# Fifteen couples instead of twelve in the second half of the value stages, with two weight sums made by accumulating DMAs

## The reference

```python
def block(args):                         # routed experts; u and v are tables of 16384 rows
    ht, et, gt = args
    act = jax.nn.gelu(jnp.einsum('td,ted->te', ht, u[et]), approximate=False)
    return jnp.einsum('te,ted->td', gt * act, v[et])
...
for layer in range(DEPTH):               # 2
    h = rms_norm(x, ...)
    x = x + (even_mix if layer % 2 == 0 else fox_mix)(h, ...)
    h = rms_norm(x, ffn_norm[layer])
    x = x + peer_ffn(h, peer_wq[layer], peer_keys[layer], peer_u[layer], peer_v[layer])
```

## Time and profile before

| | before |
|---|---|
| median of 3 runs | 2184.07 us (2183.23 to 2188.88) |
| profiled execution, its own time | 2185.0 us |
| its span | 2183.3 us, granted TensorE clock 0.999 of full |
| TensorE busy | 2169.3 us, 14158 matmuls |
| VectorE, ScalarE, GpSimd busy | 1775.3, 1257.6, 725.2 us |
| DMA | 386.11 MB, mean 177 GB/s |

### The profile page before, as it was taken

How to read it: one execution, slowest core, us unless ns; L and a number is a source line. 1 busy time by engine, 2 the same in 40 slices (tenths; PEclk the granted TensorE clock), 3 DMA queues, 4 the chain that set the end, 5 groups by cost and what they waited for, 6 DMA issues and landing times.

```text
span 2183.3 us, 42549 instructions
## 1 busy us (share of the span) xinstructions
PE 2169.3 (99%) x14158; PEld 1890.7 (87%) x14158; DVE 1775.3 (81%) x3460; ACT 1257.6 (58%) x1935; POOL 725.2 (33%) x737
## 2 busy tenths in 40 slices
PE   9999999999999999999999999999999999999999
PEld 8899888888888888888988888888888888899887
DVE  8776885888899999866678678888999997658895
ACT  6556556555444666565565555554446665566764
POOL 1506886333345100002088853324440001530000
PEclk9999999999999999999999999999999999999999
DMA  5364555555565665354455555555656654444565
GB/s 176 100 200 156 190 186 182 173 173 173 177 211 179 205 210 193 127 183 144 165 175 191 185 180 171 172 169 191 211 175 213 202 181 160 155 145 155 189 187 163
DMA packets 109836, 386.11 MB, mean 177 GB/s; under 512 B 12544, under 2 KB 15008, under 8 KB 109472
## 3 DMA queue, kind: packets, MB, share of 16 engines
q1 hardware_dynamic: 106864, 382.34, 53.0%
q10 hardware_dynamic: 2864, 2.36, 0.3%
HBM read 383.46 MB, written 1.06 MB: 176 GB/s over the span
## 4 chain that ended last, share of the span: by engine, by line
PE 92%; DVE 4%; POOL 2%; DMA 1%; ACT 1%; issue 0%; SPq 0%; ACTq 0%; DVEq 0%; POOLq 0%
PE bank L2611 24%; PE bank L2583 13%; PE bank L2663 5%; PE bank L2665 5%; PE bank L2664 5%; PE bank L2706 3%; PE bank L2707 3%; PE bank L2708 3%; PE bank L2499 3%; PE bank L2487 3%; PE bank L3070 3%; PE bank L2491 3%; PE bank L2727 2%; PE bank L2728 2%; PE bank L2729 2%; PE bank L2853 1%
## 5 line engine op out<-in xcount | busy, mean ns | idle before, releaser
L670 ACT ACTIVATE w_hi<-ring 128x1024 fp32r<-128x1024 f32 x651 | 686.9, 1056 | 435.4 <-PE bank L2665 186.8
L1378 DVE TENSOR_TENSOR w_lo<-ring,w_hi 128x1024 fp32r<-128x1024 f32 x500 | 610.2, 1223 | 109.1 <-ACT w_hi L670 109.1
L2611 PE MATMUL bank<-x_parts,w_hi 128*128 128x512 f32 x2320 | 583.1, 393 | 0.3 <-ACT w_hi L670 0.3
L2611 PEld LDWEIGHTS bank<-x_parts,w_hi 128*128 128x128 f32 x2320 | 417.0, 189 | 74.9 <-issue 0.4
L554 POOL TENSOR_TENSOR w_lo<-ring,w_hi 128x1024 fp32r<-128x1024 f32 x151 | 364.5, 2420 | 265.1 <-DVE x_parts L1363 158.5
L566 POOL COPY quads<-sco 128x32 f16 (+1 forms) x256 | 227.1, 915 | 439.7 <-DVE sco L1917 439.6
L2583 PEld LDWEIGHTS bank<-x_parts,w_lo 128*128 128x128 f32 x2368 | 324.3, 190 | 25.1 <-DVE w_lo L1378 3.0
L2583 PE MATMUL bank<-x_parts,w_lo 128*128 128x256 f32 x2368 | 335.7, 283 | 0.2 <-DVE w_lo L1378 0.2
L2663 PE MATMUL bank<-w_hi,x_parts 128*128 128x512 f32 x512 | 201.7, 394 | 0.0
L2665 PE MATMUL bank<-w_lo,x_parts 128*128 128x512 f32 x512 | 199.6, 390 | 0.0
L2664 PE MATMUL bank<-w_hi,x_parts 128*128 128x512 f32 x512 | 199.1, 389 | 0.0
(11 more groups left out here) (418 smaller groups left out, 3812.9 us busy)
## 6 DMA issues: line engine op xcount, KB each, us to landing
ring<-u_dram SPq DMA_DIRECT2D x256, 512.0 KB, 3.3
ring<-v_dram SPq DMA_DIRECT2D x208, 512.0 KB, 3.3
big<-v_dram SPq DMA_DIRECT2D x48, 512.0 KB, 4.4
ring<-up_dram SPq DMA_DIRECT2D x44, 512.0 KB, 3.5
ring<-wq_dram SPq DMA_DIRECT2D x32, 512.0 KB, 4.2
ring<-sb_in_dram SPq DMA_DIRECT2D x31, 512.0 KB, 3.3
ring<-od_in_dram SPq DMA_DIRECT2D x25, 512.0 KB, 3.3
ring<-down_dram SPq DMA_DIRECT2D x22, 512.0 KB, 4.2
```

The source lines that it names most:

```text
L670: A(w_hi[:, k % RING, :], ring[:, k % RING, :], ACT.Copy).then_inc(g["w_hi_done"], 1)
L1378: V.tensor_tensor(w_lo[:, k % RING, :], ring[:, k % RING, :], w_hi[:, k % RING, :].bitcast(F32), ALU.subtract).then_inc(g["lo_dve"], 1)
L2611: mm(dst[:, :], hi[:, rows[c]], x_both[:, c, :], start=(c == 0), stop=False, skip_group_check=True)
```

## The change

The second half is laid out as 4 plain pieces and 15 couples with two plain pieces behind each: 34 plain pieces (40 before). A raw buffer now has five blocks instead of four: SyncE loads the block B12 twice, side by side, and behind the load GpSimd issues one DMA that adds the blocks B22 and B11 onto the two copies (128 x 1024, SBUF to SBUF, `accum_op=add`). The result is T3 and T1, which VectorE made before as `t13`. For the first two couples VectorE still makes them. The signs of the sums are turned so that adding fits. VectorE's `late_sums` is split into `activation_sums` (three pieces ahead, behind the low parts) and `weight_sums` (two pieces ahead; T2 and T4, waits for the accumulating DMA). Part 0 has 2560 columns instead of 1536, part 1 has 1024 instead of 2048. TensorE raises `pair_used` for the first time after five of a couple's products instead of three. The fold begins with bank 0 released earlier and adds into the output banks as soon as each term is there. The first pair of a layer is loaded four pieces later in the first half, and some semaphores for small tables are merged.

```diff
@@ -36,11 +36,11 @@
...
 UP = 2.0 ** 14
-HEAD, COUPLED, BETWEEN, TAIL = 4, 12, 3, 0
+HEAD, COUPLED, BETWEEN, TAIL = 4, 15, 2, 0
 DIRECT = HEAD + COUPLED * BETWEEN + TAIL
...
 EARLY_SUMS = ("t13", "t2", "t4", "s1", "s3", "s2", "s4")
-SUMS = ("t13", "s1", "t2", "s3", "s2", "t4", "s4")
+SUMS = ("s1", "s3", "s2", "s4", "t2", "t4")
@@ -140,11 +140,11 @@
-        pair_raw = [big[:, b * 4 * CB:(b + 1) * 4 * CB] for b in range(2)]
-        pair_sum = [big[:, 8 * CB:12 * CB], big[:, 12 * CB:16 * CB], sco[:, 4 * CB:8 * CB]]
-        pair_sum_low = [sums_low[:, 0:4 * CB], sums_low[:, 4 * CB:8 * CB], sco_rounded[:, 4 * CB:8 * CB]]
-        pair_hi = [(parts[:, 0:3 * CB], parts[:, 3 * CB:7 * CB]), (parts[:, 13 * CB:16 * CB], sco_rounded[:, 0:4 * CB])]
-        pair_lo = [parts[:, 7 * CB:10 * CB], parts[:, 10 * CB:13 * CB]]
+        pair_raw = [big[:, b * 5 * CB:(b + 1) * 5 * CB] for b in range(2)]
+        pair_sum = [big[:, 10 * CB:12 * CB], big[:, 12 * CB:14 * CB]]
+        pair_sum_low = [sums_low[:, 2 * CB:4 * CB], sums_low[:, 4 * CB:6 * CB]]
+        pair_hi = [(parts[:, 0:5 * CB], sco_rounded[:, 5 * CB:7 * CB]), (parts[:, 10 * CB:15 * CB], sums_low[:, 6 * CB:8 * CB])]
+        pair_lo = [parts[:, 5 * CB:10 * CB], sco_rounded[:, 0:5 * CB]]
         at_pair = 3 * 2 * T
@@ -349,7 +350,12 @@
         def pair_arrived(layer, s):
-            return pair_loaded[s % 2], 32 * (layer * ((COUPLED + 1 - s % 2) // 2) + s // 2 + 1)
+            of_both = (COUPLED + 1 - s % 2) // 2
+            return pair_loaded[s % 2], 48 * (layer * of_both + s // 2 + 1)
+
+        def pair_added(layer, s):
+
+            return pair_added_to[s % 2], 16 * (layer * ((COUPLED - 1 - s % 2) // 2) + s // 2)
         def pair_free(layer, s, half=2):
@@ -470,12 +476,14 @@
             def load_pair(layer, s):
                 k, raw = couple_row(s), pair_raw[s % 2]
-                for at, row in ((0, k + 1), (PIECE, k)):
-                    sp.dma_start(raw[:, at:at + PIECE], a[f"v{layer}"][row]).then_inc(pair_loaded[s % 2], 16)
+                upper = a[f"v{layer}"][k][:, CB:2 * CB].rearrange("p (o n) -> p o n", o=1).to_broadcast([P, 2, CB])
+                sp.dma_start(raw[:, 0:2 * CB], a[f"v{layer}"][k + 1]).then_inc(pair_loaded[s % 2], 16)
+                sp.dma_start(raw[:, 2 * CB:3 * CB], a[f"v{layer}"][k][:, 0:CB]).then_inc(pair_loaded[s % 2], 16)
+                sp.dma_start(b3(raw[:, 3 * CB:5 * CB], 2), upper).then_inc(pair_loaded[s % 2], 16)
             def first_pairs(layer):
-                sp.wait_ge(g["pieces_used"], starts[f"v{layer}"] + 16)
+                sp.wait_ge(g["pieces_used"], starts[f"v{layer}"] + 20)
                 load_pair(layer, 0)
@@ -483,13 +491,13 @@
...
                 for d in range(DIRECT):
+                    sp.wait_ge(*low_bits(k0 + d - RING))
+                    load(a[f"v{layer}"][direct_row(d)], k0 + d)
                     s = pair_after(d - 2)
...
                         load_pair(layer, s + 2)
-                    sp.wait_ge(*low_bits(k0 + d - RING))
-                    load(a[f"v{layer}"][direct_row(d)], k0 + d)
@@ -607,9 +615,14 @@
...
+                for s in range(2, COUPLED):
+                    raw = pair_raw[s % 2]
+                    pool.wait_ge(*pair_arrived(layer, s))
+                    pool.dma_start(raw[:, 3 * CB:5 * CB], raw[:, CB:3 * CB], accum_op=ALU.add).then_inc(pair_added_to[s % 2], 16)
+
                 if layer == 0:
                     pool.wait_ge(g["x_ready"], 4 * 2)
-                    pool.wait_ge(g["fox_rows_spread"], 16)
+                    pool.wait_ge(g["fox_rows_spread"], 32)
                     tab = fx_tab.rearrange("p (h c t) -> p h c t", h=FH, c=3)
@@ -1048,12 +1061,12 @@
...
                     direct_chunk(d)
-                    for ahead, parts in ((3, (0,)), (2, (1,)), (1, (2, 3))):
+                    for ahead, parts in ((1, (1, 2, 3)), (2, (0,))):
                         s = pair_after(d + ahead)
...
                                 pair_part(s, part)
-                act.wait_ge(*pair_free(layer, COUPLED - 1))
+                act.wait_ge(*pair_free(layer, COUPLED - 1, 1))
                 A(pair_ends[:, 0:CB], bank[0][:, :], ACT.Copy).then_inc(g["pair_high"], 1)
@@ -1760,18 +1773,17 @@
             def couple_blocks(s):
-                raw, out, row = pair_raw[s % 2], pair_sum[s % 3], couple_row(s) * T
-                b21, b22, b11, b12 = (raw[:, j * CB:(j + 1) * CB] for j in range(4))
-                t13, t1, t2, t4 = b3(out[:, 0:2 * CB], 2), out[:, CB:2 * CB], out[:, 2 * CB:3 * CB], out[:, 3 * CB:4 * CB]
-                b12_twice = b12.rearrange("p (o n) -> p o n", o=1).to_broadcast([P, 2, CB])
+                raw, out, row = pair_raw[s % 2], pair_sum[s % 2], couple_row(s) * T
+                b21, b22, b11, t3, t1 = (raw[:, j * CB:(j + 1) * CB] for j in range(5))
+                t2, t4, t13 = out[:, 0:CB], out[:, CB:2 * CB], raw[:, 3 * CB:5 * CB]
                 a11, a21, a12, a22 = (big[:, row + j * P:row + (j + 1) * P] for j in range(4))
                 s2, s1, s4 = (act_sum[s % 2][:, j * P:(j + 1) * P] for j in range(3))
-                return {"t13": (t13, b12_twice, b3(raw[:, CB:3 * CB], 2)), "t2": (t2, b22, t1), "t4": (t4, b21, t2),
-                        "s1": (s1, a21, a22), "s3": (a21, a21, a11), "s2": (s2, s1, a11), "s4": (s4, a12, s2)}
+                return {"t13": (t13, t13, raw[:, CB:3 * CB]), "t2": (t2, b22, t1), "t4": (t4, b21, t2),
+                        "s1": (s1, a22, a21), "s3": (a21, a11, a21), "s2": (s2, s1, a11), "s4": (s4, a12, s2)}
             def block_sum(blocks, name):
-                V.tensor_tensor(*blocks[name], ALU.add if name == "s1" else ALU.subtract).then_inc(g["pair_summed"], 1)
+                V.tensor_tensor(*blocks[name], ALU.subtract if name in ("s1", "s3", "s4") else ALU.add).then_inc(g["pair_summed"], 1)
             def early_weight_sums(layer, s):
@@ -1784,26 +1796,26 @@
...
-            def late_sums(layer, s):
+            def activation_sums(layer, s):
...
                 if s >= 2:
-                    dve.wait_ge(*pair_arrived(layer, s))
                     dve.wait_ge(*pair_free(layer, s - 2))
-                    block_sum(blocks, "t13")
                 block_sum(blocks, "s1")
-                if s >= 2:
-                    dve.wait_ge(*sums_done(layer, s, "t13"))
-                    block_sum(blocks, "t2")
                 dve.wait_ge(*sums_done(layer, s, "s1"))
...
                 block_sum(blocks, "s2")
-                if s >= 2:
-                    dve.wait_ge(*sums_done(layer, s, "t2"))
-                    block_sum(blocks, "t4")
                 dve.wait_ge(*sums_done(layer, s, "s2"))
                 block_sum(blocks, "s4")
+
+            def weight_sums(layer, s):
+
+                blocks = couple_blocks(s)
+                dve.wait_ge(*pair_added(layer, s))
+                block_sum(blocks, "t2")
+                dve.wait_ge(*sums_done(layer, s, "t2"))
+                block_sum(blocks, "t4")
             def experts(layer):
@@ -2017,34 +2029,44 @@
...
                     dve.wait_ge(*pair_high(layer, 4 * s + part + 1))
-                    dst, src, high = ((pair_lo[b], pair_raw[b][:, 0:3 * CB], pair_hi[b][0]), (pair_sum_low[s % 3], pair_sum[s % 3], pair_hi[b][1]),
+                    dst, src, high = ((pair_lo[b], pair_raw[b], pair_hi[b][0]), (pair_sum_low[b], pair_sum[b], pair_hi[b][1]),
                                       (low_acts, acts, act_hi[b][:, 0:4 * P]), (act_sum_low[b], act_sum[b], act_hi[b][:, 4 * P:7 * P]))[part]
...
                     direct(d)
-                    if pair_after(d + 3) >= 0:
-                        late_sums(layer, pair_after(d + 3))
-                    for ahead, parts in ((2, (0,)), (1, (1,)), (0, (2, 3))):
+                    for ahead, parts in ((0, (1, 2, 3)), (1, (0,))):
                         s = pair_after(d + ahead)
...
                                 pair_part(s, part)
-                dve.wait_ge(*pair_high(layer, 4 * COUPLED + 1))
-                step(V.tensor_tensor(e21, bank[2][:, :], e11, ALU.add))
-                settle()
-                step(V.tensor_tensor(e12, bank[1][:, :], e21, ALU.add))
-                settle()
-                step(V.tensor_tensor(e22, bank[3][:, :], e12, ALU.add))
-                step(V.tensor_tensor(e21, bank[3][:, :], e21, ALU.add))
-                settle()
-                for j in range(4):
+                    if pair_after(d + 2) >= 2:
+                        weight_sums(layer, pair_after(d + 2))
+                    if pair_after(d + 3) >= 0:
+                        activation_sums(layer, pair_after(d + 3))
+
+                def into_output(j, op):
+
                     if j < 3:
...
                         dve.wait_ge(g["pieces_used"], k0 + DIRECT - 1)
-                    V.tensor_tensor(bank[4 + j][:, :], bank[4 + j][:, :], pair_ends[:, j * CB:(j + 1) * CB], ALU.add).then_inc(g["pair_low"], 1)
```

(17 more changed lines are left out.)

39 lines of the change are left out of this document (20 added, 19 removed).

## The result

The changed kernel takes 2213.25 us, median of 4 runs (2206.18 to 2215.2); before, 2183.8, median of 4 beside it. The ratio is 1.0123, 95% interval 1.0108 to 1.0139: 1.2% slower. The prediction was 2193 with a range from 2183 to 2212. The profiled execution is the fastest of the four, 2206.18, and its span is 2204.4 us, 21.1 above the 2183.3 of before.

What follows compares the result with a forecast made beforehand. TensorE was taken to bound the kernel, with VectorE almost as full. Matmuls saved -4.1, wait +9.6 and stage end +3.2 gave +8.7 us on the profiled 2185.0, 2193 against the 2184.07 median; range 2183 to 2212.

Steps and rivals of the forecast that it cites:

- The accumulating DMA: GpSimd's 512 KB add inside the couples' load chain: taken to land in 5.5 us, under 7.3, so costing nothing.
- 13.8 + A: Chain from raw loads through accumulation, ScalarE and VectorE to the buffer's reuse: must fit two periods, 21.1 us.
- A: Accumulating DMA's time from issue to landing: taken as 5.5 us, bounds 3.3 to 8.0, free up to 7.3.
- the accumulate is late: Rival: accumulation takes 9 us, period 11.4, +22 us, time 2215; chance 0.18.
- The wait: VectorE's activation sums wait for couple s-2, idling TensorE 0.37 us per period, 13 times a layer: +9.6 us.
- the first rival: No wait for the couple's end is felt in the periods; time 2183, chance 0.14.
- The saving: Second half of each layer: 9 matmuls fewer, 2.04 us per layer, -4.1 us in two.
- VectorE alone would thus hold the period at 10.25; all cover is gone: VectorE's work per couple period: 10.25 us against TensorE's 10.20, so no slack is left.
- The end of the stage: Fold behind the last couple: TensorE idle 1.1 us, then 0.5 more; 1.6 per layer, +3.2 us.
- The remaining edits: Raw pairs loaded four pieces later in the first half, and merged semaphores: costed at nothing.
- The descriptor rival: GpSimd cannot write descriptors while VectorE runs: period 12.2, +41 us, time 2234; chance 0.05.

Runs made afterwards that it cites:

- e1: Changed kernel with the activation sums called one iteration nearer their couple, two pieces behind couple s-2; 2213.13 us, ratio 1.0129 to the kernel before.
- e10: Changed kernel with B12 loaded once for first two couples, B11 and B12 in one 4 KB-row load, activation sums moved behind two pieces; 2197.6 us, ratio 1.0066.
- e2_noadd: Changed kernel without the accumulating DMAs, sums B11 + B12 and B22 + B12 left out; 2198.01 us, ratio 1.0059 to the kernel before.
- e8_copy: Changed kernel with GpSimd's DMA copying instead of adding, same queue, bytes and waits, T1 and T3 wrong in value; 2198.37 us, ratio 1.0061.
- e4_full: Changed kernel with B11 and B12 in one load of 4 KB rows, second B12 by itself, same bytes; 2201.05 us, ratio 1.0077.
- e5: Changed kernel without accumulating DMAs (sums with B12 left out) and with activation sums moved behind two pieces; 2184.5 us, ratio 1.0004 to the kernel before.
- e11: Changed kernel without accumulating DMAs (sums with B12 left out), activation sums moved behind two pieces, B12 loaded once for first two couples; 2181.95 us, ratio 0.9992.
- e3_early: Changed kernel with B12 loaded once for the first two couples of a layer; 2206.69 us, ratio 1.0104 to the kernel before.
- e9: Changed kernel, full computation, B12 loaded once for the first two couples, B11 and B12 in one load of 4 KB rows; 2198.86 us, ratio 1.0065.
- e12: Like e11, sums still left out, with three plain pieces ahead of the couples and one behind; 2182.31 us, ratio 0.9986 to the kernel before.
- e0_again: The changed kernel run once more, unchanged; 2209.75 us, ratio 1.0115 to the kernel before.

## Why the prediction was wrong

**What failed** is the step "The accumulating DMA ... I take 5.5 ... so nothing": it cost 7.4 us in the profiled execution. The chain was set up rightly, 13.8 + A against two periods of 21.1, but two of its links were taken too short. The three raw loads were 6.0; from the first issue to GpSimd's it is 7.9 and 7.8 in the mean of each layer. A was 5.5; from GpSimd's issue to the start of part 0 it is 6.1 and 6.2. With these the chain is 7.8 (13.8 less the 6.0) + 7.85 + 6.15 = 21.8 against two real periods of 21.27, late by 0.27 a period in the mean; the periods' excess, 7.4 in 26, is 0.28. That the two agree so closely is in part luck, since links vary by 1 to 3 us from couple to couple; that the same sum also gives the means of e1 and e10 is not. The loads' link is 1.85 too short in the prediction for three reasons: without any accumulation the three loads take 7.0 (e2_noadd), 1.0 more than my 6.0; GpSimd issues 0.3 behind the last landing; and with the accumulation beside them it is another 0.5 to 0.6. A is 0.65 too short; e8_copy shows what is the adding's own, 6.15 against 4.8 for a copy. Adding takes 2.1 times the engine time of copying: the accumulating DMAs raise the DMA share from 0.60 to 0.84, the copies to 0.72. Had the loads taken only what they take without the accumulation (7.3 to GpSimd's issue), or A its 5.5, the mean chain would be 21.25 or 21.15, just inside. Just inside isn't "nothing" either: e4_full, at 7.8 + 7.0 + 6.2 = 21.0, still has 3.4 us of late couples. The rival "the accumulate is late" had the mechanism, with a chance of 0.18, and too much of it: A = 9 was far off, 7.4 us came instead of 22.

**The wait** was right in place, sign and count: 13 times a layer, then one free period. Its size was 0.435 a period instead of 0.37, the period 10.635 instead of 10.57, +11.3 instead of +9.6; e2_noadd shows it alone, and in e5 and e11, with the sums moved, it is gone. "If no wait is felt", the first rival, falls. **The saving** was exact: 9 matmuls, e5's and e11's periods of 10.20.

**"VectorE alone would thus hold the period at 10.25; all cover is gone"** was wrong in the second half. The work was 10.27, well read. But a stage of 15 couples is short: e5's periods were 10.20 throughout, since VectorE enters with a lead and loses 1.0 us of it. A rate just over the bound costs nothing until the lead is spent.

**The end of the stage** was +1.6 a layer, 1.1 of idle and 0.5 behind it; the rows show 0.93 and 0.36, +2.6 in both layers instead of +3.2. The mechanism is right (0.62 <-DVE bank, the third output bank), its size a little too large. (By its own terms TensorE ends at 5.2 + 1.36 = 6.56, not 6.65; nothing hangs on it.)

**"The remaining edits ... I cost at nothing"** was wrong by 3.1 us in the first half: the raw loads of the first couples put 2.5 MB in front of a ring piece, and e3_early takes it away. Not the later load is at fault, which the sentence names, but the second copy of B12. I looked only at who reads the raw blocks, not at what stands behind them on SyncE's queue. **The start of the stage**, +1.0 a layer, I hadn't looked at: the activation sums' place costs once more before the first couple, since in e1, e5, e10 and e11, which move them, it is 10.88 to 10.93 (why VectorE has less lead there was not tried apart).

**The descriptor rival** falls: GpSimd's issues take 0.86 us each, with VectorE busy 140.1 of 150 us, and e8's copy lands after 4.7. So the rule that the Trainium skill has on this (SBUF — State Buffer, Who interferes with whom) held for these two-input rows.

The medians are 29.5 us apart (2213.25 and 2183.8) where 8.7 were forecast. Of the 20.8 missing, 12.4 lie between the profiled spans: late couples 7.4, wait 1.7, start 2.0, first half 3.1 and end -0.6 make 13.6, less the 1.2 by which the rest of the program was shorter. Another 7.1 is that the profiled execution is the fastest of its kernel and lies so far under its median, and 1.2 that the profiled execution of before lies above the median of before.

**Open** is what makes a couple late in one execution and not in the next, and what the 7.1 us are, since the slower executions left no trace. The record has one hint against late couples alone: the mean granted clock. The profiled execution has 0.999, the other three 0.996, 0.996 and 0.997. In the 23 executions of before that ran beside e9 to e12, the time goes with that clock: 2182.35 to 2183.43 us at 1.000, 2188.79 and 2189.05 at 0.997, some 1.9 us for each 0.001. By that (an estimate) 5 to 6 of the 7.1 us go with the lower clock, which may itself follow from waits. It isn't all of it: e0_again took 2204.78 and 2209.0 us, both at 1.000.

## What to carry to other kernels

Where a transfer adds instead of copying, book its bytes about twice in DMA engine time. Price several loads in a chain from the first issue to the last landing (here 5.2 us for two and 7.0 for three), not from the landing of one. When a stage has two limits close together (here a wait and a chain), taking away one may only show the other: run each alone and both together, and read the distance between equal rows. When a load is moved on a queue, look at what then stands behind it.

## What the runs showed of the hardware

- An accumulating DMA inside SBUF, 512 KB, landed after 6.1 us in the median (5.2 to 7.7) and moved 174 GB/s in the time that its packets took on the 16 engines; a copy of the same bytes landed after 4.7 us and moved 370 GB/s.
- Three raw loads of 1.25 MB in all landed 7.0 us after the first issue at a DMA share of 0.60, and 7.5 to 7.6 beside the accumulating DMAs, at 0.84; two of 1 MB in all 5.1 to 5.2.
- The same 1.25 MB of raw blocks took 7.0 us to the accumulation's issue with 4 KB rows for B11 and B12, and 7.9 and 7.8 with 2 KB rows, beside accumulating DMAs in both cases.
- A GpSimd tensor_tensor from SBUF held one two-input VectorE row for 2.2 us, once a couple, and itself took 2.4 to 4.65 us.
